# Paged K scored from 32x32 blocks that VectorE turns in place, in a fused decoder step

## The reference, cut to what matters

```
k_past = cache_k[page_table].reshape(nb, -1, N_HEADS, HEAD_DIM)
v_past = cache_v[page_table].reshape(nb, -1, N_HEADS, HEAD_DIM)
...
s = jnp.einsum('nqhd,nkhd->nhqk', q, k).astype(jnp.float32) * (HEAD_DIM ** -0.5)
s = s + (jnp.transpose(fq, (0, 2, 1))[:, :, :, None]
         - jnp.transpose(fk, (0, 2, 1))[:, :, None, :])
s = jnp.where(mask[None, None], s, -jnp.inf)
p = jax.nn.softmax(s, axis=-1)
return jnp.einsum('nqhk,nkhd->nqhd', p.astype(v.dtype), v)
```

## Time and profile before

| | us |
|---|---|
| median of 3 runs | 971.62 (970.4 to 973.45) |
| profiled execution | 975.04 |
| its span, first to last instruction | 973.2 |
| busy: TensorE, VectorE, ScalarE, Pool | 939.5, 486.6, 385.1, 167.4 |
| mean granted TensorE clock | 0.996 of full |

### The profile page before, as it was taken

How to read it: one execution, slowest core, us unless ns; L and a number is a source line. 1 busy time by engine, 2 the same in 40 slices (tenths; PEclk the granted TensorE clock), 3 DMA queues, 4 the chain that set the end, 5 groups by cost and what they waited for, 6 DMA issues and landing times.

```text
span 973.2 us, 23705 instructions
## 1 busy us (share of the span) xinstructions
PE 939.5 (97%) x8516; PEld 802.0 (82%) x8516; DVE 486.6 (50%) x1133; ACT 385.1 (40%) x728; POOL 167.4 (17%) x111
## 2 busy tenths in 40 slices
PE   4999999999999999999999999999999999999998
PEld 4999999999998987868768778688687686776898
DVE  5675444556355334554544544645545545445632
ACT  5333333332144443543444534535434445345210
POOL 2233444332030311102002002011020020000000
PEclk9999999999999999999999999999999999999999
DMA  7233222225343527799799798798996997987412
GB/s 233 66 87 86 86 76 75 85 65 130 120 165 103 174 55 228 254 329 341 237 360 313 249 364 290 247 376 261 315 350 237 362 323 244 365 297 249 142 44 98
DMA packets 133334, 206.41 MB, mean 212 GB/s; under 512 B 8848, under 2 KB 91457, under 8 KB 133171
## 3 DMA queue, kind: packets, MB, share of 16 engines
q1 hardware_dynamic: 121602, 198.35, 60.7%
q10 hardware_dynamic: 11168, 5.51, 2.0%
q0 software_dynamic: 528, 2.10, 0.8%
HBM read 195.29 MB, written 10.63 MB: 212 GB/s over the span
## 4 chain that ended last, share of the span: by engine, by line
PE 82%; DMA 7%; ACT 4%; DVE 4%; issue 2%; SPq 1%; ACTq 0%; DVEq 0%
PE psum L1221 40%; PE psum L1201 16%; PE psum L1270 9%; PE psum L1404 7%; PE psum L1519 4%; DMA page_ring<-in_cache_k 4%; ACT sample_scores L707 2%; DMA w_raw<-in_a_w_out 2%; PE psum L1469 1%; PE psum L1447 1%; DMA residual<-in_x_prompt 1%; PE psum L1319 1%; PE psum L1427 1%; PE psum L1449 1%; DMA page_ring<-in_cache_v 1%
## 5 line engine op out<-in xcount | busy, mean ns | idle before, releaser
L1221 PE MATMUL psum<-xn_high,w_high 128*128 128x256 f32 (+1 forms) x992 | 237.2, 318 | 2.6 <-DVE w_low L832 2.6
L1221 PE MATMUL psum<-xn_low,w_high 128*128 128x256 f32 (+1 forms) x992 | 216.4, 297 | 0.0
L1221 PE MATMUL psum<-xn_high,w_low 128*128 128x256 f32 (+1 forms) x992 | 216.3, 297 | 0.0
L1221 PEld LDWEIGHTS psum<-xn_high,w_high 128*128 128x128 f32 x992 | 163.9, 191 | 20.2 <-issue 16.6
L1221 PEld LDWEIGHTS psum<-xn_high,w_low 128*128 128x128 f32 x992 | 169.0, 191 | 0.0
L1221 PEld LDWEIGHTS psum<-xn_low,w_high 128*128 128x128 f32 x992 | 168.9, 190 | 0.0
L1201 PE MATMUL psum<-constants,page_ring 128*128 128x128 f32 x1024 | 137.5, 277 | 7.7 <-DMA page_ring<-in_cache_k 6.5
L1201 PEld LDWEIGHTS psum<-constants,page_ring 128*128 128x128 f32 x1024 | 114.8, 141 | 35.1 <-issue 33.4
L501 POOL TENSOR_TENSOR w_raw<-w_raw,gains 128x1024 f32<-128x1024 f32 x32 | 60.8, 1899 | 338.9 <-DMA w_raw<-in_b_w_in 220.7
L1009 DVE COPY k_turned_odd<-psum 128x512 f32<-128x512 f32 x64 | 44.2, 691 | 93.5 <-PE psum L1201 93.5
L832 DVE TENSOR_TENSOR w_low<-w_raw,w_high 128x1024 fp32r<-128x1024 f32 x32 | 51.4, 1606 | 72.6 <-ACT w_high L565 72.6
(11 more groups left out here) (236 smaller groups left out, 1420.2 us busy)
## 6 DMA issues: line engine op xcount, KB each, us to landing
page_ring<-in_cache_k SPq DMA_DIRECT2D x128, 512.0 KB, 5.6
page_ring<-in_cache_v SPq DMA_DIRECT2D x128, 512.0 KB, 4.8
w_raw<-in_a_w_in SPq DMA_DIRECT2D x30, 512.0 KB, 4.1
suffix<-suffix_scratch SPq DMA_DIRECT2D x32, 256.0 KB, 4.8
w_raw<-in_b_w_in SPq DMA_DIRECT2D x16, 512.0 KB, 6.2
w_raw<-in_kv_w SPq DMA_DIRECT2D x16, 512.0 KB, 6.1
w_raw<-in_a_w_out SPq DMA_DIRECT2D x4, 1024.0 KB, 5.1
f_broad<-f_scratch SPq DMA_DIRECT2D x8, 512.0 KB, 6.2
```

What stands on the lines that cost most here:

```text
L1221: mm = pe.matmul(PS[:, bank + h, 0:c.stop - c.start], w[:, k, :], x[:, k, c], start=(k == 0 and n == 0), stop=(k == KT - 1 and n == 2))
```

## The change

K pages are no longer turned by TensorE. VectorE turns each page in its slot, in blocks of 32x32 (one `transpose` a page, in place), so that in each group of 32 partitions r the block of columns c holds dimensions 32c to 32c+31 of the tokens 32r to 32r+31. Scores are then taken per unit of four pages: for each of 32 blocks of dimensions c and each of four partition groups r one matmul of 32 rows, 32 query columns and 128 key columns at tile (32r, 32j). Row group r writes bank C0 + r, so a unit fills the four banks C0, C1, OP and OS, and the key order in them is by r. `q_blocks` (QD) holds the queries for that, for each head half a block of 32 columns with zeros in the columns of other heads; it lies over `w_high_b`. Ahead of the loop TensorE spreads q over the four partition groups (`q_quarters`, 16 matmuls), ScalarE and VectorE copy it out, and Pool fills QD for each pass.

The rest follows from it: the suffix is stored in the permuted key order (`CSP`) and read with a stride of 4; V pages are loaded with their rows in that order (row 32r + n to partition 4n + r); V's projection goes to banks T0 and T1, the sum of squares too; a slot of the first eight pages is freed by whole units (`unit_scored`); the K and V projections stand in an inner loop of two passes around the units; V rows are turned ahead of K rows, and the next V weights' high half follows on ScalarE behind the copies. Pool makes the three low halves of a pass (`low_p`).

The core of the diff, the renamed counters left out:

```diff
+GROUP = 4
+NG = NPG // GROUP
...
+    WHB = place("w_high_b", [P, KT, SLAB], F32R)
+    QD = place("q_blocks", [P, 2 * H, 32], over=at["w_high_b"])
     PTS = place("p_turned", [P, NPG, P])
-    KTS.append(place("k_turned_odd", [P, KT, 2 * PAGE], over=at["p_turned"]))
...
+            if n < NPG:
+                src = kpages[bass.ds(page, 1), :, :].rearrange("a p n -> (a p) n")
+            else:
+                src = vpages[bass.ds(page, 1), :, :].rearrange("a (r n) d -> n (a r) d", r=4)
+            sp.dma_start(ring[:, n % RING, :], src).then_inc(b_page[n % RING], 16)
...
                     if n < NPG:
-                        sp.wait_ge(b_t1, 24 * i + n + 1)
+                        if n % GROUP == 0:
+                            sp.wait_ge(b_su, NG * i + n // GROUP + 1)
...
+        def low_p(n, slot):
+
+            pool.wait_ge(b_high, n + 1)
+            pool.tensor_tensor(WL[:, slot, :, :], WR[:, slot, :, :], WH[:, slot, :, :].bitcast(F32),
+                               ALU.subtract).then_inc(b_split, 1)
...
+        def block_queries(b):
+
+            own = QN[:, bass.ds(b, 1), 0:2 * H * NQ].rearrange("p a (j x f q) -> p x (a j) f q", x=4, f=2, q=NQ)
+            to = QD[:, :, :].rearrange("p (j x f) n -> p x j f n", x=4, f=2)
+            for x in range(4):
+                ins = pool.tensor_copy(to[:, x, :, :, NQ * x:NQ * x + NQ], own[:, x])
+            ins.then_inc(b_qd, 1)
+
+        pool.wait_ge(b_proj, 2)
+        pool.memset(QD[:, :, :], 0.0).then_inc(s_qz, 1)
         pool.wait_ge(q_out, KT)
-        pool.tensor_copy(QC[:, :, :], QZ[:, 0, :, :]).then_inc(b_qc, 1)
         pool.tensor_copy(QT[:, :], QF[:, 0, 0:SEQ]).then_inc(b_qt, 1)
+        pool.wait_ge(s_qne, 4)
+        pool.wait_ge(s_qz, 1)
+        block_queries(0)
...
             scale_b(1, 6 + 2 * i, G_B)
+            low_p(KT + 3 * i + 2, 1)
             if not last:
                 scale_b(0, 6 + i, G_KV)
             pool.wait_ge(b_rr, i + 1)
             pool.tensor_tensor(KN_T[:, :], KN_T[:, :], RR[:, :], ALU.mult).then_inc(b_normed, 1)
             if not last:
+                low_p(KT + 3 * i + 3, 0)
                 scale_b(1, 7 + 2 * i, G_KV)
-                pool.wait_ge(b_c1, 8 * i + 4)
-                pool.tensor_copy(QC[:, :, :].rearrange("p k n -> p (k n)"),
-                                 QZ[:, bass.ds(i + 1, 1), :, :].rearrange("p a k n -> p (a k n)")).then_inc(b_qc, 1)
-                pool.wait_ge(b_c0, 8 * i + 8)
-                pool.wait_ge(b_c1, 8 * i + 8)
+                pool.wait_ge(b_su, NG * (i + 1))
+                block_queries(i + 1)
+                low_p(KT + 3 * i + 4, 1)
...
+        def turn_pages(i, ks):
+            for k in ks:
+                dve.wait_ge(b_page[k % RING], (4 * i + k // RING + 1) * 16)
+                dve.transpose(ring[:, k % RING, :], ring[:, k % RING, :]).then_inc(b_kt, 1)
+
+        turn_pages(0, range(2))
         query(KT - 1, 1)
+        turn_pages(0, range(2, GROUP))
...
+                dve.wait_ge(b_sfx[u % 2], (2 * i + u // 2 + 1) * 16)
+                dve.wait_ge(b_su, NG * i + u + 1)
+                dve.memset(TINY[0:1, 32 + u:33 + u], 0.0)
+                out, later = (z.rearrange("p (m r) -> p r m", r=4)
+                              for z in (SS[:, u * 512:(u + 1) * 512], SFX[:, u % 2, :]))
+                dve.tensor_tensor_reduce(out, PS[:, C0:OS + 1, 0:P], later, 1.0, NEG, ALU.add, ALU.max,
+                                         TINY[:, 4 + u:5 + u]).then_inc(b_suf, 1)
+
+            turn_pages(i, range(4, 8))
+            add_suffix(0)
+            dve.wait_ge(b_proj, KT + 3 * i + 1)
+            pr, sa = both(D0)
+            gk = GAIN[:, G_K:G_K + 1]
+            dve.tensor_scalar(prompt2(KN_T[:, 0:SEQ]), pr, gk, None, ALU.mult)
+            dve.tensor_scalar(KN_T[:, SEQ:TOK], sa, gk, None, ALU.mult).then_inc(b_ddve, 1)
+            turn_pages(i, range(8, 11))
+            add_suffix(1)
+            turn_pages(i, range(11, 16))
+            add_suffix(2)
+            add_suffix(3)
...
-            assert t1[0] == 24
+                turn_pages(i + 1, range(2))
             dve.wait_ge(b_po, i + 1)
             dve.wait_ge(b_sz, i + 1)
             dve.tensor_tensor(SQ[:, 0:SEQ], PS[:, OP, :], SZ[:, 0:SEQ], ALU.mult).then_inc(b_gf, 1)
...
             dve.tensor_tensor(gl, SQ[:, 0:SEQ], gh.bitcast(F32), ALU.subtract).then_inc(b_gl, 1)
+            if not last:
+                turn_pages(i + 1, range(2, GROUP))
...
+        for c in range(4):
+            for r in range(4):
+                mm = pe.matmul(PS[32 * r:32 * r + 32, T0 + c, :].rearrange("p (m n) -> p m n", m=KT),
+                               CT[:, C_ID + 32 * c:C_ID + 32 * c + 32], QF[:, :, SEQ:TOK],
+                               start=True, stop=True, tile_position=(0, 32 * r))
+        mm.then_inc(s_qn, 1)
...
+            def unit_scores(a, u):
+
+                pe.wait_ge(b_kt, NPG * i + 2 * GROUP * a + GROUP * (u + 1))
+                pe.wait_ge(b_suf, NG * i + 2 * a + u)
+                pe.matmul(PS[:, OS, 511:512], IDB[:, :], CMB[:, 0:1], start=True, stop=True)
+                for xf in range(8):
                     for j in range(4):
+                        c = 8 * j + xf
+                        for r in range(4):
+                            mm = pe.matmul(PS[32 * j:32 * j + 32, C0 + r, 0:P], QD[32 * r:32 * r + 32, c, :],
+                                           ring[32 * r:32 * r + 32, GROUP * u:GROUP * (u + 1), 32 * c:32 * c + 32],
+                                           start=(xf == 0), stop=(xf == 7), tile_position=(32 * r, 32 * j))
+                mm.then_inc(b_su, 1)
+
+            def pieces(a, ks):
+                with pe.If(a):
+                    if ks[0] == 0:
+                        pe.wait_ge(b_t0f, 8 * i)
+                        pe.wait_ge(b_t1f, 8 * i)
+                    for k in ks:
+                        mm = piece(0, k, T0)
+                    if ks[-1] == KT - 1:
+                        mm.then_inc(b_proj, 1)
+                with pe.Else():
+                    if ks[0] == 0:
+                        pe.wait_ge(b_split, KT + 3 * i + 2)
+                        pe.wait_ge(b_sz, i)
+                    for k in ks:
+                        mm = piece(1, k, D0)
+                    if ks[-1] == KT - 1:
+                        mm.then_inc(b_proj, 1)
+
+            with pe.Fori(0, 2) as a:
+                pieces(a, range(0, 4))
+                pe.wait_ge(b_qd, i + 1)
+                pe.wait_ge(s_qne, 4)
+                pe.wait_ge(b_c0f, 4 * i)
+                pe.wait_ge(b_c1f, 4 * i)
+                pe.wait_ge(b_sot, i)
+                pe.wait_ge(b_gf, i)
+                unit_scores(a, 0)
+                pieces(a, range(4, 8))
+                unit_scores(a, 1)
+
+            pe.wait_ge(b_dact, 2 * i + 2)
+            pe.matmul(PS[:, T0, 0:NS], CT[:, C_ONESB:C_ONESB + P], SQ[:, SEQ:TOK], start=True, stop=True)
+            pe.matmul(PS[:, T1, :], CT[:, C_ONESB:C_ONESB + P], SQ[:, 0:SEQ], start=True, stop=True).then_inc(b_ss, 1)
```

254 lines of the change are left out of this document (94 added, 160 removed).

## The result

The changed kernel takes 1061.0 us (median of five runs, 1046.8 to 1062.8), the kernel before 970.4 us beside it: a ratio of 1.087, 95% interval 1.080 to 1.095. The ratio is that of the means of the fast executions, 1055.8 and 971.1 us; the changed kernel's spread over 16 us, so a difference between two kernels is given by these means where it matters. The forecast was 940 us with a range of 915 to 1038.

What follows compares the result with a forecast made beforehand. TensorE was taken to bound the loop, DMA close behind at its head. 5.2 us a pass saved less 1.0 for clock, 7 x 4.2 + 3 = 32 us off 975, 3.4 above the median: 940 us, range 915 to 1038.

Steps and rivals of the forecast that it cites:

- What bounds the kernel, what is removed: Heads loop: TensorE bounds it, DMA close behind at its head; page transposes and K scores removed, 21.6 of 66.67 us a pass.
- The units: K scores on TensorE: four units a pass, 256 instructions each at 9.6 ns, 2.5 us a unit (bounds 1.7 and 3.55).
- that row shows no floor of issue: Unit price: the nearest row's 13.9 ns an instruction was read as an upper limit, since array time alone asks 13.4 ns.
- The rival at 25 ns: Score units: issue-bound at 25 ns an instruction, 6.4 us a unit, V 7.8 us late, 1035 us in all; chance 10%.
- The turns: K page turns on VectorE: 1.15 us a page, sixteen turns 18.4 us, VectorE under 40 us a pass.
- The stall of 4.4 us before unit 0: Head of a pass: TensorE done at 636.1 waits 4.4 us for page 3, turned at 640.5.
- The layout of the pass: Pass step by step: unit 3 ends at 662.75, V starts at 675.3 instead of 680.5, 5.2 us a pass saved.
- Clock: TensorE behind the 4.4 us stall each pass: a stretch at lower clock, charged 1.0 us a pass (0 to 2).
- Ahead of the loop: Spreading q 3.4 us plus 3 us waiting, 6.5 us lost, against 5.2 + 4.4: pass 0 gains about 3 us.
- Edits at nothing: Pool's low halves, Q blocks, permuted suffix and extra query product: hidden beside other work, no cost.
- The low halves on Pool: Pool, 17% busy, takes 1.9 us each against VectorE's 1.23; the tightest has about 2 us to spare; no cost.
- in another row order that leaves the rows of 4 KB whole: V page loads in the V part: pages come as before, the part (680.47 to 700.27) keeps its length.

Runs made afterwards that it cites:

- e7_units_narrow: e5_units_looped with 64 instead of 128 columns per score matmul (2 of a unit's 4 pages): 1017.1 us.
- e2_pad_looped: The kernel before plus 257 one-column matmuls ahead of each pass's first scores, 256 of them in an inner loop of 4 turns over 64: 1040.7 us.
- e5_units_looped: The changed kernel with each score unit written as half of its 128 matmuls, gone through twice in an inner loop: 1019.6 us.
- e11_turn_small: e5_units_looped with VectorE turning only the first 32 of each page's 1,024 columns: 987.0 us.

## Why the prediction was wrong

Two steps failed: the price of a unit was set below the row nearest to it, and code written out was taken as free. The second weighs more.

*What bounds the kernel, what is removed.* Right: TensorE bounded it, and its busy time fell by 35.5 us. The gain that was not there lies in idle time.

*The units.* The first step that failed is "that row shows no floor of issue, only that it is not above 13.9". It was the nearest price there was. A unit's instruction costs 14.0 ns (12.9 read as that row was), near the bound from above, and a unit 3.58 us in place of 2.5. The row nearest in kind (32-column weights, a load for each matmul) stood at 13.9; the value taken was between it and an array time that does not bind, for e7_units_narrow keeps four fifths of the price with half the columns. 4.3 us a pass more, and the prediction itself says that each unit also holds back the next pages. The rival at 25 ns, taken from the Trainium skill (TensorE: Matmul & The Clock Gate, "Wait — 56ns, not 53.3ns?"), falls for tiles; but one-column matmuls with whole-array loads in e2_pad_looped cost 25.7 ns each, which agrees with that page.

*The turns.* Right: 1.23 us on average, 6.87 us for six in a row in e5_units_looped, 1.15 each. The stall of 4.4 us before unit 0 is there as 4.84 us, once the fetch no longer hides it. The layout of the pass behind it was too short: against the end of the V part unit 0 starts at 8.9 us (forecast 7.6), unit 1 at 17.3 (13.3), unit 2 at 26.4 (20.9), unit 3 at 35.1 (27.35), and it ends at 39.1 in place of 29.85. Of these 9.2 us 6.5 are the units' own length (16.5 us in place of 10, one of them at low clock), 1.2 the later start, and 1.5 lie between the units, 1.0 of them ahead of the last: pages 12 to 15 land 10.5 us after the first of them is asked for (678.51 to 689.06; 8.7 was forecast), and a suffix pass takes 1.08 us, not 0.75. Behind unit 3 the changed kernel needs 14.0 us to the first V matmul (forecast 12.55), 2.4 of them Pool's hold.

*Clock.* Right for the stall that it was charged to: behind the wait for page 3, unit 0 of e5_units_looped takes 4.95 us where unit 1 takes 3.83, 1.1 us (1.0 was charged). In the changed kernel the fetch's stalls bring the lower level twice a pass, 2.4 and 2.7 us in the pass shown.

*Loop and branches.* This is the step that put the time beyond the forecast's range, and no rival had it. The prediction counted instructions as time on TensorE and never as code to be fetched, although the two units written out add 509 instructions to the loop body net, and the trace of before showed an instruction queue that was silent in the loop. The fetch costs 36 us by the mean times (41 by the medians, 29 by the profiled spans), and would cost more if a wait for turns did not lie under it. Half a microsecond for each start of an inner round, also not counted, is 8.1 us in e5_units_looped.

*Ahead of the loop.* A gain of 3 us was forecast for pass 0; by the end of its V part the changed kernel is 12 us late. Spreading q took 5.01 us, not 3.4, behind a wait of 3.21; in pass 0 too the first two units break off (1.47 and 2.34 us), and Pool holds VectorE. The rest was not taken apart.

*Edits at nothing.* "The low halves on Pool" was wrong: slack of Pool was checked, its hold on VectorE was not; 10 us by the p part (1.47 us in seven passes), 11 by the mean times. The V pages "in another row order that leaves the rows of 4 KB whole" were wrong by 5 us; the row order had been named among what could go wrong.

*Sum.* By the mean times: fetch 36, turns 34, Pool 11, V rows 5, together 86 us, measured one at a time, beside the 85 us by which the kernel is slower. They are not proved to add up, and part of the turns' price was in the forecast. That the rest of the change gained next to nothing can be followed in e11_turn_small, which has neither fetch nor whole turns. TensorE's work alone (21.6 us off each pass, 14.3 us of units on it) would take its K part from 42.0 to 34.7 us; it is 39.4. Of these 38 us in eight passes TensorE waits 12.7 for suffix passes, 7.7 for pages and their short turns and 7.6 at the starts of inner rounds. The sign would have turned without the fetch: e5_units_looped, which does the rest of the change (its units run their first half twice), is 5% slower than before.

## What to carry to other kernels

Count the instructions of an engine's loop body, weight loads too, before unrolling more work into it, and look at the instruction queue: if it is silent in the loop now, that silence is part of the time. Price many small matmuls by the nearest row with as narrow weights and a load for each, not by the array's time, and ask of a stall that goes what was waiting under it. Work given to Pool is free only if VectorE has no short copies between SBUF tiles there that something waits for.
